# Paged keys and values of a decode step fetched as joined rows of 512 bytes, keys transposed by identity products in column halves, and the prompt outputs' split moved in on-chip memory

## The chip, the cores and the metric

One Trainium2 chip, one of its cores. The metric is the device time of one execution in microseconds. The program uses TensorE (PE, its weight loads PEld), VectorE (DVE), ScalarE (ACT), GpSimd (POOL) and SyncE (SP), which here only issues transfers. SP and POOL each issue transfers to a queue of their own; the core's 16 DMA engines serve both.

## The reference: what is computed

One layer of a hybrid decoder, for a prompt of 512 tokens and for 8 decode batches of 4 new tokens each, all in float32:

```python
hp = pre_mix(xp, ...)            # LN(alpha*x + 0.5*SwiGLU1(x)), 1024 wide, hidden 2816
qa, ka, va, qb, kb, vb, qi, ki, wi = project(hp, w_in[i], ...)
...
o_b = dsa_step(qb, kb, vb, qi, wi, ki, cache_b[i], page_table, bias_b)
xs = post_mix(hs, o_a, o_b, w_out[i], ...)   # w_out, LN, SwiGLU2, LN, gated embedding
```

For the decode tokens, mixer A (12 heads) attends over a cache of 2048 rows per batch (7 blocks of 128 keys are read, `cache_a`), and mixer B (4 query heads, one shared key and value head of 64) attends over those 256 of the past positions that an indexer picks. Mixer B's past is in pages: `cache_b` holds rows of 192 floats, key (64), value (64), indexer key (64), 128 rows to a page, 16 pages to a batch, found by `page_table`. The kernel reads the keys and values of all 128 pages and masks what the indexer left out.

## The kernel before, in words

All five engines run programs written out by hand, synchronised by semaphores; each executes its instructions strictly in the order written. The stages are: the first SwiGLU, the projection (with the indexer's scores), prompt attention (it ends at about 731 us), decode attention (731 to 921 us), `w_out`, the second SwiGLU, the gate. The change lies in decode attention, which has two halves.

**The key half** (731 to 846 us). Mixer A's keys come in 56 blocks `n` of 128 rows by 3072 bytes, 14 for each of four groups `a`. SP issues their loads into a ring of 5 slots (`load_keys`, L489 to L492). After each load from the sixth on it issues one page of mixer B, and two after every fourth, until its 64 pages are out (L518 to L522). POOL issues the 64 pages of odd number one after another (L691 to L692). Both use `load_kv_page` (L375 to L380), which first reads the page's number into a register and then issues one transfer of 64 KB, keys to one half of the tile `kv_b_pages` and values to the other, in runs of 256 bytes. For each block, PE transposes it with six products with the identity (L1998), ACT copies the result to SBUF (L929, L930), and PE takes 12 products with the queries (L1981). PE's loop (L1992 on) transposes block `n` ahead of the scores of block `n - 1`. On DVE the selection of the top 256 runs beside this, cut in pieces with the logits of group `a` after piece `a` (L1432 to L1453):

```python
            for a in range(4):
                if a == 0:
                    list_rounds(0, 16)
                elif a == 1:
                    list_rounds(16, 32)
                    merge_lists()
                    left_per_chunk()
                elif a == 2:
                    mark_rounds(0, 32)
                ...
                dve.wait_ge(S["ka_sc"], 15 * (a + 1))
```

ACT has the softmax exponentials of group `a` in the same loop (`exp_a`, L918, after blocks 18, 32 and 46), so that ACT, and then PE, wait there for DVE's logits.

**The value half** (846 to 917 us). It has 32 steps `v`. Each takes two value blocks of mixer A out of a ring of 7 slots (`values_a`, L2111 on, products on L2124); SP issues a load when two slots are free (L494 to L502). Steps 0 to 15 begin with `transposed_b(v)` (L2005 to L2016): page group `v`, that is page `v` of the 8 batches, is transposed, 4 products of 128x128 with the identity. ACT copies it (`keys_b`, L942), PE takes the scores. Steps 19 to 23 transpose mixer B's probabilities, and steps 24 to 26 are `values_b` (L2085 to L2101): 17 groups of 4 products of 32 output rows, page values against probabilities.

**The prompt's outputs.** Before `w_out` each of the 8 chunks of the prompt's attention output is cast to a rounded part on DVE (`prompt_high`, L1476 to L1479) and the rest is subtracted on POOL (L694 to L699). Both results lie over the pages: the rounded part over the keys (so it waits until all page groups are transposed, `kb_t`), and the last chunk of the rest over a piece of the values (so it waits for `vb_all`, the end of `values_b`). POOL's next work is the first `w_rest` of `w_out` (L557), which waits for ACT's `w_high`; that waits for the last value step (`va_pair`).

Of the kernel before, what the change touches and what calls it, by code (L numbers as in the profile page):

```python
# [22 lines left out]
F32R = mybir.dt.float32r  # L23
# [22 lines left out]
T = SEQ + NDEC  # L46
# [73 lines left out]
def build_program(nc, x_t, p_t, cache_a, cache_b, page_table, ln, kidx_g, kidx_b, w, rel_bias,  # L120
                  rel_rows, consts, onehots, patterns, mask_new, toeplitz, y_t, kv_a_t, a_sample, kv_b_t, ki_b):
    ctx = ExitStack()
    with ctx:
# [4 lines left out]
        def sb(name, shape, dt=F32, at=None):  # L128
# [86 lines left out]
        OT = sb("attn_out_t", [128, KD, T], at=y_at)  # L215
        OH_ = sb("attn_out_high", [128, KD, T], F32R, at=h_at)
        OL_ = sb("attn_out_rest", [128, KD, T], F32R, at=h_at + KD * T * 4)
        SC = sb("idx_scores", [128, CHUNK_COLS + 8], at=e_at)
# [25 lines left out]

        KVP = sb("kv_b_pages", [128, 2, DEC_BATCH * PAGES, HD], at=h_at)
        STA = sb("logits_a", [128, 4, ALL_A], at=h_at + 65536)
# [26 lines left out]
            topk_dec_done kb_t kb_sb kb_sc b_logits b_kept b_max b_exp  # L273
            pt_ps2 pt_a pt_d vb_all ob_sb oa_sb ob_t va_used va_pair ot_done o_tail
            oh_ready o_ready dve_step""".split()
# [99 lines left out]
        def load_kv_page(eng, q):  # L375

            g, b = q // DEC_BATCH, q % DEC_BATCH
            page = eng.value_load(PAGE_IDS[0:1, b * PAGES + g:b * PAGES + g + 1], min_val=0, max_val=cache_b.shape[0] - 1)
            eng.dma_start(KVP[:, :, q, :], cache_b[bass.ds(page, 1), :, 0:2 * HD].rearrange("o p (s n) -> (o p) s n", s=2)  # L379
                          ).then_inc(kv_in[g // 4 + 4 * (q % 2)], 16)  # L380
# [170 lines left out]
        def _(pool):  # L551
# [142 lines left out]
            for c in range(KD):  # L694
                pool.wait_ge(S["oh_ready"], c + 1)
                if c == KD - 1:
                    pool.wait_ge(S["vb_all"], 1)
                nc.gpsimd.tensor_tensor(OL_[:, c, 0:SEQ], OT[:, c, 0:SEQ], OH_[:, c, 0:SEQ].bitcast(F32), ALU.subtract  # L698
                                        ).then_inc(S["o_ready"], 1)  # L699
# [290 lines left out]
        def _(dve):  # L990
# [485 lines left out]
            def prompt_high(c):  # L1476

                dve.wait_ge(S["kb_t"], PAGES)
                v.tensor_copy(OH_[:, c, 0:SEQ], OT[:, c, 0:SEQ]).then_inc(S["oh_ready"], 1)  # L1479

# [100 lines left out]
        def _(pe):  # L1581
# [423 lines left out]
            def transposed_b(g):  # L2005

                if g % 4 == 0:
                    for queue in range(2):
                        pe.wait_ge(kv_in[g // 4 + 4 * queue], 16 * 2 * DEC_BATCH)
                if g >= 2:  # L2010
                    pe.wait_ge(S["kb_sb"], g - 1)
                for p in range(4):
                    last = tr(BANK[2 + g % 2][:, 128 * p:128 * p + 128],
                              KVP[:, 0, DEC_BATCH * g + 2 * p:DEC_BATCH * g + 2 * p + 2, :].rearrange("p b n -> p (b n)"),
                              IDENT)
                last.then_inc(S["kb_t"], 1)  # L2016
# [68 lines left out]
            def values_b(g0, g1):  # L2085
# [5 lines left out]
                for g in range(g0, g1):  # L2091
                    for p in range(4):
                        if g < PAGES:
                            val = KVP[:, 1, DEC_BATCH * g + 2 * p:DEC_BATCH * g + 2 * p + 2, :]
                            probs = PTB[:, g, 32 * p:32 * p + 32]
                        else:
                            val, probs = VBN[:], PTB[0:32, g, 32 * p:32 * p + 32]
                        last = mm(BANK[7][32 * p:32 * p + 32, 0:128], probs, val, start=g == 0, stop=g == PAGES,
                                  skip_group_check=True)
                if g1 == PAGES + 1:  # L2100
                    last.then_inc(S["vb_all"], 1)  # L2101
# [223 lines left out]
```

## Time and profile before

| | |
|---|---|
| time, median of 3 runs | 1476.61 us (1473.54 to 1477.29) |
| the profiled execution's own time | 1477.71 us |
| its span in the trace | 1476.1 us |
| mean granted TensorE clock | 0.972 |
| PE / DVE / ACT / POOL busy | 94% / 38% / 30% / 42% |
| moved by the DMA engines | 269.83 MB, mean 183 GB/s |
| SP's queue / POOL's queue, share of the 16 engines | 51.8% / 2.6% |

PE is busy 94% of the time over the whole program, but the shares are means over stages: in the key half of decode attention PE is busy some three quarters, and other resources decide when the stage ends. The chain of waits over the whole program gives PE 80% and DVE 7%.

### The profile page before, as it was taken

To read this page: it belongs to the slowest core of one execution; us is meant where nothing else is said; L and a number is where in the kernel's file an instruction comes from. 1 tells how busy PE (TensorE), PEld (TensorE's weight loads), DVE (VectorE), ACT (ScalarE), POOL (GpSimd) and SP (SyncE) were. 2 spreads that over 40 slices of the span, in tenths; PEclk is the share of its full clock that TensorE was granted. 3 is DMA by queue.
4 is the path that set the end of the run, shared out by engine and by line. 5 is a ranking of instruction groups with operands and counts; after the bars stand their busy time and mean duration, and the time that the engine had idled before them with its cause. 6 is when DMAs were issued, how large, how long until landed. Compare 5 with 4: busy or idle time off the path is not lost.

```text
span 1476.1 us, 30731 instructions
## 1 busy us (share of the span) xinstructions
PE 1380.6 (94%) x12059; PEld 1272.4 (86%) x12059; DVE 556.1 (38%) x1340; ACT 449.4 (30%) x833; POOL 626.9 (42%) x431
## 2 busy tenths in 40 slices
PE   6999999999989999997876897979999999999988
PEld 6999999999979879965554565969999999999888
DVE  5222222200252346777889524162222222110454
ACT  2122222211252343256643431154222222211441
POOL 6344333455465645221455004534444333544542
PEclk9999999999999999999998998989999999999999
DMA  6299756766355523331299898425565657665221
GB/s 229 79 258 313 271 191 212 252 230 212 117 179 179 150 83 104 133 111 44 61 286 283 247 308 302 143 91 189 172 229 175 220 187 268 218 222 178 72 69 46
DMA packets 95774, 269.83 MB, mean 183 GB/s; under 512 B 36305, under 2 KB 36690, under 8 KB 95160
## 3 DMA queue, kind: packets, MB, share of 16 engines
q1 hardware_dynamic: 89000, 255.34, 51.8%
q0 software_dynamic: 5632, 10.50, 2.6%
q10 hardware_dynamic: 1040, 2.62, 1.2%
q8 instruction: 66, 1.08, 0.3%
q14 instruction: 36, 0.29, 0.1%
HBM read 259.78 MB, written 109.10 MB: 250 GB/s over the span
## 4 chain that ended last, share of the span: by engine, by line
PE 80%; DVE 7%; ACT 4%; POOL 4%; issue 3%; DMA 2%; SPq 1%; ACTq 0%; DVEq 0%; POOLq 0%
PE bank L1588 22%; PE bank L1592 21%; PE bank L1590 21%; POOL w_rest L557 2%; DVE idx_scores L1430 2%; PE bank L2124 2%; PE bank L1941 1%; PE bank L1931 1%; DMA cache_a_ring<-in_cache_a 1%; PE bank L1953 1%; ACT y L785 1%; PE bank L1636 1%; PE bank L1998 1%; DVE idx_scores_left L1376 1%; POOL x_rest L567 1%
## 5 line engine op out<-in xcount | busy, mean ns | idle before, releaser
L557 POOL TENSOR_TENSOR w_rest<-w_raw,w_high 128x1024 fp32r<-128x1024 f32 (+2 forms) x162 | 417.8, 2579 | 593.5 <-ACT w_high L728 592.6
L728 ACT ACTIVATE w_high<-w_raw 128x1024 fp32r<-128x1024 f32 (+2 forms) x162 | 183.5, 1134 | 789.9 <-PE bank L1592 746.5
L1588 PE MATMUL bank<-x_high,w_high 128*128 128x272 f32 x1856 | 388.9, 291 | 15.7 <-POOL x_rest L567 11.6
L1592 PE MATMUL bank<-x_high,w_rest 128*128 128x272 f32 x1856 | 385.4, 289 | 0.0
L1590 PE MATMUL bank<-x_rest,w_high 128*128 128x272 f32 x1856 | 384.1, 289 | 0.0
L1588 PEld LDWEIGHTS bank<-x_high,w_high 128*128 128x128 f32 x1856 | 292.5, 189 | 24.4 <-issue 18.6
L1590 PEld LDWEIGHTS bank<-x_rest,w_high 128*128 128x128 f32 x1856 | 293.0, 189 | 0.0
L1592 PEld LDWEIGHTS bank<-x_high,w_rest 128*128 128x128 f32 x1856 | 291.3, 190 | 0.0
L1032 DVE SCALAR_TENSOR_TENSOR hidden<-silu_gate,bank 128x272 f32<-128x272 f32 x88 | 34.6, 434 | 394.1 <-ACT silu_gate L746 394.1
L1588 PE MATMUL bank<-hidden_high,w_high 128*128 128x272 f32 x616 | 127.8, 289 | 0.0
L1592 PE MATMUL bank<-hidden_high,w_rest 128*128 128x272 f32 x616 | 127.5, 288 | 0.0
L1590 PE MATMUL bank<-hidden_rest,w_high 128*128 128x272 f32 x616 | 127.0, 288 | 0.0
L1588 PEld LDWEIGHTS bank<-hidden_high,w_high 128*128 128x128 f32 x616 | 97.0, 188 | 0.2
L1590 PEld LDWEIGHTS bank<-hidden_rest,w_high 128*128 128x128 f32 x616 | 96.8, 189 | 0.0
L1592 PEld LDWEIGHTS bank<-hidden_high,w_rest 128*128 128x128 f32 x616 | 96.2, 189 | 0.0
L1053 DVE SCALAR_TENSOR_TENSOR y<-y,bank 128x272 f32<-128x272 f32 x42 | 16.5, 434 | 207.6 <-PE bank L1592 179.4
L1998 PE MATMUL bank<-consts_sb,cache_a_ring 128*128 128x128 f32 x336 | 54.4, 304 | 18.5 <-DMA cache_a_ring<-in_cache_a 17.5
L1998 PEld LDWEIGHTS bank<-consts_sb,cache_a_ring 128*128 128x128 f32 x336 | 40.2, 153 | 32.1 <-DMA cache_a_ring<-in_cache_a 24.8
L379 POOL DMA_DIRECT2D kv_b_pages<-in_cache_b x64 | 46.2, 721 | 40.4 <-issue 40.4
L1036 DVE CAST hidden_high<-hidden 128x544 f32 (+1 forms) x44 | 49.1, 1116 | 7.8 <-DVE hidden L1032 3.5
L698 POOL TENSOR_TENSOR attn_out_rest<-attn_out_t,attn_out_high 128x512 fp32r<-128x512 f32 x8 | 10.5, 1329 | 91.8 <-DVE attn_out_high L1479 91.8
L929 ACT ACTIVATE k_a_t<-bank 128x512 f32<-128x512 f32 x56 | 33.4, 597 | 52.7 <-PE bank L1998 52.7
(303 smaller groups left out, 1815.3 us busy)
## 6 DMA issues: line engine op xcount, KB each, us to landing
out_a_sample<-in_cache_a SPq DMA_DIRECT2D x73, 1344.0 KB
w_raw<-in_w_wi SPq DMA_DIRECT2D x88, 512.0 KB, 5.0
cache_a_ring<-in_cache_a SPq DMA_DIRECT2D x112, 384.0 KB, 5.1
w_raw<-in_w_wo SPq DMA_DIRECT2D x32, 704.0 KB, 5.4
w_raw<-in_w_w_in SPq DMA_DIRECT2D x26, 512.0 KB, 3.9
w_raw<-in_w_gate SPq DMA_DIRECT2D x8, 640.0 KB, 3.9
bias_toeplitz<-rev_bias POOLq DMA_DIRECT2D x32, 128.0 KB, 2.7
kv_b_pages<-in_cache_b POOLq DMA_DIRECT2D x64, 64.0 KB, 4.1
```

Source lines behind the costliest of these rows:

```text
L379: eng.dma_start(KVP[:, :, q, :], cache_b[bass.ds(page, 1), :, 0:2 * HD].rearrange("o p (s n) -> (o p) s n", s=2)).then_inc(kv_in[g // 4 + ...
L557: nc.gpsimd.tensor_tensor(WL[:, s, 0:tiles, :], RAW[:, slot, 0:tiles, :], WH[:, s, 0:tiles, :].bitcast(F32), ALU.subtract).then_inc(S["lo_ ...
L728: nc.scalar.activation(WH[:, s, 0:tiles, :], RAW[:, slot, 0:tiles, :], ACT.Copy).then_inc(S["hi_ready"], 1)
L929: nc.scalar.activation(KTA[:, n % 2, 0:512], BANK[b0][:, :], ACT.Copy)
L1032: last = v.scalar_tensor_tensor(half(HF, s, n), half(SG, s, n), 0.5, BANK[4 * s + 2 + n][:, 0:HALF], ALU.mult, ALU.mult)
L1036: v.tensor_copy(HH[:, bass.ds(c, 1), :], HF[:, s:s + 1, :]).then_inc(S["hh_done"], 1)
L1430: own.done(v.match_replace(SC[:], TOP[:, 8 * r:8 * r + 8], SC[:], PASSED))
L1588: mm(banks[n][:, 0:HALF], wh, xh[n], start=start, stop=False)
L1590: mm(banks[n][:, 0:HALF], wh, xl[n], start=False, stop=False)
L1592: last = mm(banks[n][:, 0:HALF], wl, xh[n], start=False, stop=stop)
L1998: last = tr(BANK[2 * (n % 2) + c // 4][:, 128 * (c % 4):128 * (c % 4) + 128], AR[:, n % KEY_RING, 128 * c:128 * c + 128], IDENT)
L2124: last = mm(BANK[a % 2][32 * j:32 * j + 32, 128 * s:128 * s + 128], probs, val, start=k == 0 and i < 4, stop=k == 7, skip_group_check=True)
```

## The change

Each page is now fetched as 128 rows of 512 bytes, key and value together, so the tile has keys and values side by side for every page. A pair of pages' keys is then no longer one block of 128 columns, and the transposition takes each page by itself: 8 products of 64 columns in place of 4 of 128, the two pages of a pair to the lower and the upper 64 rows of the bank. The values of a pair are read as two runs of 64. The parts of the prompt's output lie elsewhere: the rounded part over mixer A's and B's logits (free once they are transposed, `pt_ps2` at 8, at 10 for the last two chunks), the rest over the first 34 pages of the tile (free once `values_b` has done its first six page groups, the new semaphore `vb_part`, on which all 8 chunks wait).

```diff
-        OH_ = sb("attn_out_high", [128, KD, T], F32R, at=h_at)
-        OL_ = sb("attn_out_rest", [128, KD, T], F32R, at=h_at + KD * T * 4)
+        OH_ = sb("attn_out_high", [128, KD, T], F32R, at=h_at + 65536)
+        OL_ = sb("attn_out_rest", [128, KD, T], F32R, at=h_at)
-        KVP = sb("kv_b_pages", [128, 2, DEC_BATCH * PAGES, HD], at=h_at)
+        KVP = sb("kv_b_pages", [128, DEC_BATCH * PAGES, 2 * HD], at=h_at)
-            eng.dma_start(KVP[:, :, q, :], cache_b[bass.ds(page, 1), :, 0:2 * HD].rearrange("o p (s n) -> (o p) s n", s=2)
+            eng.dma_start(KVP[:, q, :], cache_b[bass.ds(page, 1), :, 0:2 * HD].rearrange("o p n -> (o p) n")
                           ).then_inc(kv_in[g // 4 + 4 * (q % 2)], 16)
             for c in range(KD):
                 pool.wait_ge(S["oh_ready"], c + 1)
-                if c == KD - 1:
-                    pool.wait_ge(S["vb_all"], 1)
+                pool.wait_ge(S["vb_part"], 1)
             def prompt_high(c):
-                dve.wait_ge(S["kb_t"], PAGES)
+                dve.wait_ge(S["pt_ps2"], 8 if c < 6 else 10)
                 for p in range(4):
-                    last = tr(BANK[2 + g % 2][:, 128 * p:128 * p + 128],
-                              KVP[:, 0, DEC_BATCH * g + 2 * p:DEC_BATCH * g + 2 * p + 2, :].rearrange("p b n -> p (b n)"),
-                              IDENT)
+                    for e in range(2):
+                        last = mm(BANK[2 + g % 2][64 * e:64 * e + 64, 128 * p:128 * p + 128],
+                                  KVP[:, DEC_BATCH * g + 2 * p + e, 0:HD], IDENT, start=True, stop=True)
-                            val = KVP[:, 1, DEC_BATCH * g + 2 * p:DEC_BATCH * g + 2 * p + 2, :]
+                            val = KVP[:, DEC_BATCH * g + 2 * p:DEC_BATCH * g + 2 * p + 2, HD:2 * HD]
+                if g0 == 0:
+                    last.then_inc(S["vb_part"], 1)
```

How the instructions stand on two engines. First TensorE at the start of the value half (L2082 transposes mixer A's probabilities, L2013 the page keys, L2124 or L2125 takes mixer A's values; the size is that of the output). Before:

```order
L2082 MATMUL bank<-consts_sb,logits_a 32x128
L2013 MATMUL bank<-consts_sb,kv_b_pages 128x128 [waits kv_in4,kv_in0,vnew_in]
L2013 MATMUL bank<-consts_sb,kv_b_pages 128x128 x3
L2124 MATMUL bank<-cache_a_ring,probs_a_t 32x128 [waits ar_in1,ar_in2,pt_d,pt_a]
L2124 MATMUL bank<-cache_a_ring,probs_a_t 32x128 x11
```

With the change:

```order
L2081 MATMUL bank<-consts_sb,logits_a 32x128
L2013 MATMUL bank<-consts_sb,kv_b_pages 64x128 [waits kv_in4,kv_in0,vnew_in]
L2013 MATMUL bank<-consts_sb,kv_b_pages 64x128 x7
L2125 MATMUL bank<-cache_a_ring,probs_a_t 32x128 [waits ar_in1,ar_in2,pt_d,pt_a]
L2125 MATMUL bank<-cache_a_ring,probs_a_t 32x128 x11
```

The place and the waits are the same; 4 products have become 8 of half the rows, in each of 16 steps.

Second, POOL from its last page to the start of `w_out`. Before:

```order
L378 TENSOR_LOAD page_ids
L378 ISA x2
L379 ISA
L379 DMA kv_b_pages<-in_cache_b 128x2x64
L698 TENSOR_TENSOR attn_out_rest<-attn_out_t,attn_out_high 128x512 [waits oh_ready] x7
L698 TENSOR_TENSOR attn_out_rest<-attn_out_t,attn_out_high 128x512 [waits vb_all,oh_ready]
L557 TENSOR_TENSOR w_rest<-w_raw,w_high 128x1024 [waits hi_ready]
```

With the change:

```order
L378 TENSOR_LOAD page_ids
L378 ISA x2
L379 ISA
L379 DMA kv_b_pages<-in_cache_b 128x128
L697 TENSOR_TENSOR attn_out_rest<-attn_out_t,attn_out_high 128x512 [waits vb_part,oh_ready] x8
L557 TENSOR_TENSOR w_rest<-w_raw,w_high 128x1024 [waits hi_ready]
```

The transfer has one run per row in place of two, and the seven subtractions that waited for DVE alone now also wait for the first part of `values_b`.

## Rows read from the trace of the kernel before

**Rows 1.** Chain of waits, 700 to 960 us: start us, us, what.
```profile
745.89 6.77 DMA cache_a_ring<-in_cache_a
...
761.46 0.69 DVE logits_a L1448
...
829.31 0.60 DVE logits_a L1448
```
**Rows 2.** Timeline of DVE, 754 to 765 us: start us, us, instruction [idle before <-releaser].
```profile
756.54 0.71 DVE L1376 MATCH_REPLACE8 idx_scores_left<-topk_lists,idx_scores_left 128x544 f32<-128x544 f32 x1
761.46 0.69 DVE L1448 CUSTOM_DVE_ANT_0 logits_a<-bank,bias_a 128x512 f32<-128x512 f32 x1 [4.21 <-PE bank L1988]
```
**Rows 3.** Timeline of PE, 728 to 762 us: start us, us, instruction [idle before <-releaser].
```profile
740.52 0.87 PE L1998 MATMUL bank<-consts_sb,cache_a_ring 128*128 128x128 f32 x6 [0.95 <-DMA cache_a_ring<-in_cache_a]
...
752.70 1.54 PE L1998 MATMUL bank<-consts_sb,cache_a_ring 128*128 128x128 f32 x6 [2.40 <-DMA cache_a_ring<-in_cache_a]
...
759.63 0.88 PE L1998 MATMUL bank<-consts_sb,cache_a_ring 128*128 128x128 f32 x6
```
**Rows 4.** Timeline of SP's queue, 725 to 850 us.
```profile
736.33 0.70 SPq L492 DMA_DIRECT2D cache_a_ring<-in_cache_a  x1
...
750.52 1.60 SPq L379 DMA_DIRECT2D kv_b_pages<-in_cache_b  x2
752.16 0.58 SPq L492 DMA_DIRECT2D cache_a_ring<-in_cache_a  x1
...
837.95 0.47 SPq L492 DMA_DIRECT2D cache_a_ring<-in_cache_a  x1
```
**Rows 5.** Instructions by tile: durations ns min/median/max, first and last start us.
```profile
L379 POOL DMA_DIRECT2D kv_b_pages<-in_cache_b x64: 720/720/747, 732.9 to 809.6; - x64
L379 SPq DMA_DIRECT2D kv_b_pages<-in_cache_b x64: 377/378/848, 734.7 to 839.2; - x64
...
L355 SPq DMA_DIRECT2D idx_pages_ring<-in_cache_b x64: 337/338/672, 444.7 to 581.6; - x64
...
L355 POOL DMA_DIRECT2D idx_pages_ring<-in_cache_b x64: 534/537/700, 463.9 to 590.4; - x64
```
**Rows 6.** Stretches: PE, PEld, DVE, ACT, POOL busy, PEclk, DMA share, GB/s.
```profile
735.00:740.00 5.00, 4.57 (x66) 3.21 (x58) 4.76 (x11) 3.41 (x8) 2.89 (x4) 1.00 0.75 216
...
745.00:750.00 5.00, 3.66 (x51) 2.62 (x51) 4.79 (x10) 1.98 (x5) 3.29 (x5) 1.00 1.05 284
750.00:755.00 5.00, 2.60 (x26) 1.74 (x20) 4.76 (x12) 1.36 (x4) 2.18 (x3) 0.71 0.95 293
...
885.00:890.00 5.00, 4.41 (x72) 3.09 (x75) 2.61 (x9) 1.16 (x2) 0.00 (x0) 1.00 0.99 348
```
**Rows 7.** Timeline of ACT, 801 to 833 us.
```profile
830.73 1.07 ACT L920 ACTIVATE logits_a<-logits_a,small 128x928 f32<-128x928 f32 x1 [4.70 <-DVE small L1452]
```
**Rows 8.** Timeline, 725 to 760 us: half-array and full-array products in prompt attention.
```profile
727.31 0.66 PE L1953 MATMUL bank<-probs_t,kv_b_tok 128*64 128x128 f32 x8
...
727.90 1.09 PE L1941 MATMUL bank<-consts_sb,logits 128*128 128x128 f32 x8
```
**Rows 9.** Timeline of PE, 846 to 884 us.
```profile
849.42 0.66 PE L2013 MATMUL bank<-consts_sb,kv_b_pages 128*128 128x128 f32 x4
```
**Rows 10.** Timeline of all engines, 884 to 924 us.
```profile
898.92 5.46 POOL L698 TENSOR_TENSOR attn_out_rest<-attn_out_t,attn_out_high 128x512 fp32r<-128x512 f32 x4 [2.92 <-DVE attn_out_high L1479]
...
911.42 1.26 POOL L698 TENSOR_TENSOR attn_out_rest<-attn_out_t,attn_out_high 128x512 fp32r<-128x512 f32 x1 [0.36 <-DVE attn_out_high L1479]
...
917.73 2.34 POOL L557 TENSOR_TENSOR w_rest<-w_raw,w_high 128x1024 fp32r<-128x1024 f32 x1 [5.05 <-ACT w_high L728]
```
**Rows 11.** Instructions by tile: mixer B's values.
```profile
L2098 PE MATMUL bank<-kv_b_pages,probs_b_t x128: 272/273/273, 899.4 to 905.4; 128*32 128x128 f32 x128
```
**Rows 12.** Landing of the keys' and values' loads.
```profile
DMA to landing us min/median/max: 3.2/5.1/6.9
```
**Rows 13.** Timeline of PE, 884 to 924 us: the end of the value half.
```profile
913.59 1.51 PE L2124 MATMUL bank<-cache_a_ring,probs_a_t 128*32 128x128 f32 x24 [2.81 <-DMA cache_a_ring<-in_cache_a]
```

More of the change, by code:

```diff
@@ L273, in build_program @@
             topk_dec_done kb_t kb_sb kb_sc b_logits b_kept b_max b_exp
-            pt_ps2 pt_a pt_d vb_all ob_sb oa_sb ob_t va_used va_pair ot_done o_tail
+            pt_ps2 pt_a pt_d vb_part vb_all ob_sb oa_sb ob_t va_used va_pair ot_done o_tail
             oh_ready o_ready dve_step""".split()
```

## The prediction

> **What bounds the kernel now.** The page sends one to decode attention, since the change touches nothing else; I read the chain of waits there first. It runs through one landing of mixer A's keys, then through DVE's top-256 selection from 761 to 829 us, broken only by the logits of each group [rows 1]. So three places could matter: the key loads up to 761 us, DVE's own chain after them, and the tail of the value half.
>
> The first place has the only slack I can find for this change. DVE ends its first 16 list rounds at 756.54 + 0.71 = 757.25 us and then stands idle 4.21 us for the scores of group 0 [rows 2]. PE is late with them because it waits for keys: block 6 starts 0.95 us late, block 11 has waited 2.40 us [rows 3]. After that gap PE's blocks 11 to 13 run at the lower clock level (1.2 GHz for part of the time; the granted clock of 750 to 755 us is 0.71 [rows 6], and six transposes take 1.54 us in place of 0.88 [rows 3]). Two things hold the keys back. SP's queue has a pace of its own: keys 6 and 14 are issued at 736.33 and 752.16 us, 1.98 us a block, since most of a page's issue is the read of its number (two pages take 1.60 us) [rows 4]. And the DMA engines are full: share 0.75 at 735 us, 1.05 at 745 us, for 284 GB/s, while the value half, which moves only long rows, gets 348 GB/s at share 0.99 [rows 6]. Pages in runs of 256 bytes are the difference in the mix.
>
> **The change part by part.**
>
> *Runs of 512 bytes.* Half the descriptors. On POOL a page costs 720 ns with 256 runs and 537 ns with 128 [rows 5]; on SP 378 and 338 ns [rows 5]. SP issues 12 pages ahead of key 14, so this key is issued 12 x 0.04 = 0.5 us sooner, at 751.7 us. Landing: key 6, issued while the engines were at 0.75, was used 740.52 - 736.33 = 4.2 us later [rows 3, 4]; the median of all ring loads is 5.1 us, the fastest 3.2 us [rows 12]. From PE's start on block 14 to DVE's logits it takes 761.46 - 759.63 = 1.83 us at the full clock [rows 2, 3], because block 13's scores come after block 14's transposes. So DVE would start at 751.7 + landing + 1.83:
> - landing 3.2 us: 756.7 us, before DVE asks. All 4.2 us go.
> - landing 4.2 us: 757.7 us, gain 3.7 us.
> - landing 5.1 us: 758.6 us, gain 2.8 us.
> - nothing lands sooner and the low clock stays: only the 0.5 us of issue.
>
> I take between the two middle rows, 4.6 us and a gain of 3.3 us: the mix becomes cheaper, so I expect the queue to stay nearer to its state of 735 us, and the gap of 2.40 us, with the low clock behind it, to shrink. Bounds: 0.5 and 4.2 us.
>
> The Trainium skill, DMA: Bandwidth & Descriptors, Specifications, puts the least transfer at line rate at 512 bytes and says that below it the engine does a read-modify-write. By it the whole penalty of the pages goes and the 4.2 us are taken; no row shows a run of 512 bytes, and the pair of shares above only agrees in direction.
>
> *Faster issue on POOL.* It gives 64 x 0.183 = 11.7 us back to an engine that waits for nobody there. But its pages press on the engines sooner: one each 0.96 us in place of 1.14 us, so 26 in place of 22 over the 25 us to 757 us. Four pages are 262 KB, at 284 GB/s 0.9 us of engine time taken from the keys. I count it inside the landing times above, and keep 0.9 us as the bound of a loss.
>
> *What is late next.* A shift of DVE at 757 us carries on only if nobody else is late. From 761 to 829 us DVE itself is the chain, without a gap [rows 1], and ACT waits for it 4.70 us before the exponentials of group 2 at 830.73 us [rows 7], with PE behind ACT. SP ends its last key at 837.95 us [rows 4]; it saves 64 x 0.04 = 2.6 us on its pages, and what it waited for PE after 801 us shrinks with DVE's shift, so it keeps step with 3.3 us. The half-clock restart of PE after 831 us stays, as the stall that causes it stays. The value half then starts 3.3 us sooner, with the same loads and the same work.
>
> *Transposes in halves.* 16 groups, 4 full-array products replaced by 8 half-array ones, at the same place. Four full ones are busy 0.66 us [rows 9], eight in alternating halves 0.66 us, eight full ones 1.09 us [rows 8]: two halves together cost one full product, (1.09 - 0.66) / 4 = 0.11 us. Cost 0, within 16 x 0.05 = 0.8 us either way. If the halves did not overlap, each group would cost 4 x 0.11 = 0.43 us more, 6.9 us in all, on PE, which is the bound of that stretch.
>
> The Trainium skill speaks against this edit. TensorEngine Tiling (Array Packing), Gotcha 2, says that tiling by columns excludes fast weight load and, for fp32, the transpose mode, and TensorE: Matmul & The Clock Gate, Terms, calls that mode four times faster for fp32. By that rule the eight would be four times dearer than the four. In the rows just named the trace does not agree: full transposes and half-array products move the same columns in the same time.
>
> *Page values as two runs of 64.* Another layout of the moving operand, at 128 products that take 6.0 us in all [rows 11]. No row shows such an operand; if it halved their rate it would cost up to 6 us in steps 24 to 26, beside a tail in which PE waits for landings anyway (2.81 us in one place [rows 13]). I take 0, bounds 0 to 3.
>
> *The split of the prompt outputs.* DVE's casts: at their place in DVE's program the eighth transposition group of mixer A has been taken already, the new wait costs nothing. POOL's eight subtractions now start at `vb_part`, about 901 us, the end of the first part of `values_b`. Before, four took 5.46 us from 898.92 us, and the last ended at 912.68 us [rows 10]. Now six in a row take 6 x 1.37 = 8.2 us, to 909.2 us, and the seventh and eighth wait for DVE as before, until 912.7 us. Behind them is the first `w_rest`, which starts at 917.73 us after 5.05 us of idling [rows 10]. Cost 0 with 5 us in hand; DVE's casts at 899 us lose their neighbour on POOL, which nobody waits for.
>
> *Sum.* 1477.7 - 3.3 = 1474.4 us against the profiled execution's own time. That lies 1.1 us over the median of the three runs, so against the median it is 1473.3; I say 1473.5 us. What a measurement of this kernel can tell from no change is 0.3%, 4.4 us.
>
> **The rivals.**
> 1. *More than DVE's wait comes back.* With the wait gone (4.2 us), the halves a little faster (0.8 us) and PE never late in the key half, one stretch of low clock less might show at its end: at the lower level six transposes cost 0.66 us more (1.54 for 0.88 [rows 3]) and the scores of a block some 0.4 us by the same ratio, so two blocks 2 us. Gain 7 us, 1469.5 us. For it: each of the key waits stems from full engines. Against: DVE's chain caps what the key half can give at 4.2 us, and a PE that is early stalls longer, so its clock falls all the same.
> 2. *SP's pace is the whole matter.* Landings are 4 to 5 us whatever the engines' load, or POOL's sooner pages take what the longer runs give (0.9 us), or the engines take two keys' worth of 256 bytes as fast as one of 512, so that the edit does not do what it says. Then 0.5 us of gain less 0.9 us of loss: 1476 to 1477 us. For it: 1.98 us a block is SP's pace. Against: the gap of 2.40 us is no matter of pace, since key 11 was issued in time.
> 3. *The halves do not overlap, slower.* Place: L2013, PE's bound stretch from 847 to 883 us. Price: 6.9 us if the products queue, 16 x 0.7 = 11 us if their weight loads show too. The tail is full of transfers, so nothing of it is taken back there. With the gain of the key half taken off, 1480 to 1485 us. It decides slower from 8 us of price on, or with no gain in the key half from 4.4 us. For it: the weight of each half changes with every product, and the values' strided operand adds to it. Against: prompt attention has the same pattern at the same size [rows 8].
>
> **How the numbers follow.** The forecast (gain 1.5 to 4.8 us) has 0.55, rival 1 0.24, rival 2 0.13, rival 3 0.08. The predicted time is the forecast's. The range is 1470.5 to 1477.5 us: the lower end takes in the full 4.2 and the 0.8 us (1471.6) and the near part of rival 1, the upper end rival 2 with its 0.9 us of loss; rival 3 and the far part of rival 1 are left out. Faster by over 0.3%: rival 1 and the forecast's edge, 0.27. Within 0.3%: the rest of the forecast and rival 2, 0.65. Slower: 0.08.
>
> **What would show it.** POOL's page issue at about 540 ns and SP's at 340 ns; DVE's wait before the logits of group 0 down from 4.21 to about 1 us; the gap before block 11 below 1 us, with the granted clock of 750 to 760 us near 1; the value half starting about 3 us sooner; L2013 eight products in 0.6 to 0.7 us. The prediction is wrong if the wait of group 0 stays above 3 us, if the groups of L2013 last 1 us or more, if ACT's wait before 830 us vanishes (then SP or PE has become the bound), or if POOL's last subtraction ends after the first `w_high`.

## The result and the profile after

The change runs in 1481.26 us, the median of 8 runs (1478.29 to 1483.89), against 1475.63 us (1472.56 to 1477.29) for the kernel before in 8 runs on the same chip. The ratio is 1.0039, with a 95% interval of 1.0023 to 1.0054, so the change is **slower**, by 5.6 us between the medians. The predicted 1473.5 us had the wrong sign, and the range (to 1477.5 us) missed. The profiled execution took 1482.50 us, its span is 1480.8 us, the mean granted clock 0.971.

I cut decode attention at three points of PE's timeline in each trace: the first transposition of mixer A's keys, the first transposition of its probabilities (the end of the key half), and the first product of `w_out`. Before they stand at 731.62, 846.25 and 921.08 us, after at 732.47, 844.31 and 924.65 us. The key half went from 114.63 to 111.84 us, the value half from 74.83 to 80.34 us. So the loss lies in the value half. The 2.8 us of the key half look like the gain that was predicted, but kernels with the same key half differ by as much from one execution to the next (the table further down), so this pair of traces alone doesn't show it.

PE's timeline after, at the start of the value half (start us, us, instruction):

```profile
845.33 1.09 PE L2013 MATMUL bank<-consts_sb,kv_b_pages 128*64 128x128 f32 x16
...
847.49 1.09 PE L2013 MATMUL bank<-consts_sb,kv_b_pages 128*64 128x128 f32 x16
848.51 0.86 PE L2125 MATMUL bank<-cache_a_ring,probs_a_t 128*32 128x128 f32 x24
```

The number behind the x, the count of rows, is what I had not reckoned with. A page group has 8 products in the program and 16 rows in the trace, and it takes 848.51 - 847.49 = 1.02 us. The group of before, 4 products in 4 rows, takes 850.01 - 849.42 = 0.59 us to the next start; that is the row of [rows 9] and the one behind it:

```profile
850.01 0.86 PE L2124 MATMUL bank<-cache_a_ring,probs_a_t 128*32 128x128 f32 x24
```

The views of the instructions by tile (durations in ns, minimum, median and maximum, then the first and the last start) say it for all 16 groups. First before, then after:

```profile
L2013 PE MATMUL bank<-consts_sb,kv_b_pages x64: 272/273/330, 847.2 to 882.5; 128*128 128x128 f32 x64
```

```profile
L2013 PE MATMUL bank<-consts_sb,kv_b_pages x256: 272/273/323, 845.3 to 887.4; 128*64 128x128 f32 x128
...
L2097 PE MATMUL bank<-kv_b_pages,probs_b_t x128: 272/273/273, 906.0 to 912.3; 128*32 128x128 f32 x128
L379 POOL DMA_DIRECT2D kv_b_pages<-in_cache_b x64: 544/547/568, 733.7 to 808.2; - x64
L379 SPq DMA_DIRECT2D kv_b_pages<-in_cache_b x64: 336/338/947, 735.5 to 837.5; - x64
```

64 products left 64 rows, 128 products left 256. The stretch from the first to the last group grew from 35.3 to 42.1 us, by 6.8 us or 0.43 us a group. The 128 value products with their strided operand have the same 273 ns. The page issues fell from 720 and 378 ns [rows 5] to 547 and 338 ns, as forecast from the index pages' rows.

POOL's timeline, before and after, shows what the shorter issue is worth (each row with the idle time before it):

```profile
738.97 0.72 POOL L379 DMA_DIRECT2D kv_b_pages<-in_cache_b  x1 [0.45 <-issue]
740.12 0.72 POOL L379 DMA_DIRECT2D kv_b_pages<-in_cache_b  x1 [0.42 <-issue]
```

```profile
738.64 0.55 POOL L379 DMA_DIRECT2D kv_b_pages<-in_cache_b  x1 [0.60 <-issue]
739.79 0.55 POOL L379 DMA_DIRECT2D kv_b_pages<-in_cache_b  x1 [0.61 <-issue]
```

One page each 1.15 us in both at this place: what the issue gives, the gap ahead of it takes. Over all 64 pages the mean is 1.22 us before and 1.18 us after (first to last start 76.7 and 74.5 us). The wait of DVE for the scores of group 0, 4.21 us before [rows 2], is 2.27 us after:

```profile
760.37 0.69 DVE L1447 CUSTOM_DVE_ANT_0 logits_a<-bank,bias_a 128x512 f32<-128x512 f32 x1 [2.27 <-PE bank L1987]
```

By stretches, the granted clock (the first number after the last bracket, 0.81 and 0.85), the busy share of the DMA engines and their GB/s:

```profile
750.00:755.00 5.00, 3.12 (x34) 2.07 (x32) 4.76 (x11) 1.61 (x4) 2.51 (x5) 0.81 0.98 311
755.00:760.00 5.00, 5.00 (x81) 3.82 (x78) 3.00 (x6) 2.42 (x7) 2.42 (x5) 0.85 0.96 311
```

Two signs that the prediction had named did not come: this clock was to be near 1, and the wait ahead of key block 11 below 1 us, where it was 1.88 us (2.40 us before):

```profile
752.86 1.36 PE L1997 MATMUL bank<-consts_sb,cache_a_ring 128*128 128x128 f32 x6 [1.88 <-DMA cache_a_ring<-in_cache_a]
```

At the other end, POOL's subtractions came later than before and still had room:

```profile
907.68 7.43 POOL L697 TENSOR_TENSOR attn_out_rest<-attn_out_t,attn_out_high 128x512 fp32r<-128x512 f32 x6 [98.89 <-PE bank L2097]
...
917.20 1.26 POOL L697 TENSOR_TENSOR attn_out_rest<-attn_out_t,attn_out_high 128x512 fp32r<-128x512 f32 x1 [0.36 <-DVE attn_out_high L1478]
921.30 2.34 POOL L557 TENSOR_TENSOR w_rest<-w_raw,w_high 128x1024 fp32r<-128x1024 f32 x1 [2.84 <-ACT w_high L727]
```

The first `w_rest` still waits for ACT's `w_high`, 2.84 us, not for POOL's own work.

### The profile page after: what moved, and what is told of

Read it like the earlier page. It is cut to its first block, busy times and chain, and to the rows that moved or that the text cites. A ratio compares the mean times of both kernels' runs of the same rounds, so it can differ in the third digit from the quotient of the medians.

```text
span 1480.8 us, 31122 instructions
## 1 busy us (share of the span) xinstructions
PE 1389.1 (94%) x12251; PEld 1283.3 (87%) x12251; DVE 553.5 (37%) x1340; ACT 449.7 (30%) x833; POOL 615.9 (42%) x431
## 4 chain that ended last, share of the span: by engine, by line
PE 81%; DVE 8%; POOL 4%; ACT 3%; issue 2%; DMA 2%; SPq 0%; ACTq 0%; DVEq 0%; POOLq 0%
PE bank L1587 22%; PE bank L1591 21%; PE bank L1589 21%; POOL w_rest L557 2%; DVE idx_scores L1429 2%; PE bank L2125 2%; DMA cache_a_ring<-in_cache_a 1%; PE bank L1940 1%; PE bank L1635 1%; PE bank L2013 1%; PE bank L1952 1%; PE bank L1930 1%; PE bank L1636 1%; PE bank L1637 1%; PE bank L1997 1%
## 5 line engine op out<-in xcount | busy, mean ns | idle before, releaser
L379 POOL DMA_DIRECT2D kv_b_pages<-in_cache_b x64 | 35.0, 547 | 49.1 <-issue 49.1
```

The lines of the kernel that those rows point to most:

```text
L379: eng.dma_start(KVP[:, q, :], cache_b[bass.ds(page, 1), :, 0:2 * HD].rearrange("o p n -> (o p) n")).then_inc(kv_in[g // 4 + 4 * (q % 2)], 16)
```

## The experiments

Times are medians; each ratio is against runs of the kernel before on the same chip, with its 95% interval. A gain or a loss in us is worked out from the ratio, unless two medians are named; with few runs the two can differ.

**The three parts, each alone.** These four ran together, beside 29 runs of the kernel before at 1475.32 us.

`e1_halves_alone`: the kernel before with its transpositions in halves, from the old layout.

```diff
-                    last = tr(BANK[2 + g % 2][:, 128 * p:128 * p + 128],
-                              KVP[:, 0, DEC_BATCH * g + 2 * p:DEC_BATCH * g + 2 * p + 2, :].rearrange("p b n -> p (b n)"),
-                              IDENT)
+                    for e in range(2):
+                        last = mm(BANK[2 + g % 2][64 * e:64 * e + 64, 128 * p:128 * p + 128],
+                                  KVP[:, 0, DEC_BATCH * g + 2 * p + e, :], IDENT, start=True, stop=True)
```

> The kernel before, with its own page layout and 256-byte runs; only the 64 full transposes become 128 products of 64 columns with the identity. Theory A (a plain float32 product runs as two passes and a transpose as one, so a group costs 1.02 us for 0.59 us; 16 x 0.43 = 6.9 us on TensorE, of which the value half takes back some 1.4 us): slower by 5.5 to 6.9 us, DVE's wait for group 0 still 4.2 us, L2013 with 256 rows. Rival B (the products are hidden, the loss comes from the moved outputs or the strided values): within 1.5 us of before.

Measured: 1484.51 us (6 runs), 1.0049 [1.0031, 1.0067], 7.2 us slower with an interval of 4.6 to 9.9 us; the medians lie 9.2 us apart. The trace has 256 rows for the 128 products, from 845.7 to 887.8 us, 42.1 us as in the change. The whole loss is this one edit. DVE's wait for group 0 was 3.73 us here.

`e2_rows_alone`: the change, with four full-array transposes of a whole page's row of key and value in place of the halves. It leaves out the keys of the odd pages and keeps the strided values and the moved outputs.

```diff
-                    for e in range(2):
-                        last = mm(BANK[2 + g % 2][64 * e:64 * e + 64, 128 * p:128 * p + 128],
-                                  KVP[:, DEC_BATCH * g + 2 * p + e, 0:HD], IDENT, start=True, stop=True)
+                    last = tr(BANK[2 + g % 2][:, 128 * p:128 * p + 128],
+                              KVP[:, DEC_BATCH * g + 2 * p, :], IDENT)
```

> The changed kernel, but with 4 full transposes to a group again, each of the 128 neighbouring columns of the even page (its keys and its values); the odd pages' keys are left out, so the time and not the output is that of joined rows with the old cost on TensorE. Theory A: faster than before by 2 to 3.5 us, the value half from the transposes of mixer A's probabilities to w_out as long as before (74.8 us). Rival B: as slow as the change, or no gain over before.

Measured: 1474.12 us, 0.9988 [0.9977, 0.9999], 1.8 us faster. Instructions by tile:

```profile
L2012 PE MATMUL bank<-consts_sb,kv_b_pages x64: 272/273/330, 844.5 to 879.9; 128*128 128x128 f32 x64
```

The stretch is 35.4 us again. So the fetch in rows of 512 bytes, with the two other parts beside it, is a gain of about half the size I had put on it. The interval runs from 0.1 to 3.4 us: the sign is just clear of noise, the size is not well known.

`e3_moved_alone`: the kernel before with only the prompt outputs moved and their waits changed.

```diff
-        OH_ = sb("attn_out_high", [128, KD, T], F32R, at=h_at)
-        OL_ = sb("attn_out_rest", [128, KD, T], F32R, at=h_at + KD * T * 4)
+        OH_ = sb("attn_out_high", [128, KD, T], F32R, at=h_at + 65536)
+        OL_ = sb("attn_out_rest", [128, KD, T], F32R, at=h_at)
...
-                if c == KD - 1:
-                    pool.wait_ge(S["vb_all"], 1)
+                pool.wait_ge(S["vb_part"], 1)
...
-                dve.wait_ge(S["kb_t"], PAGES)
+                dve.wait_ge(S["pt_ps2"], 8 if c < 6 else 10)
```

> The kernel before with only the prompt outputs' split moved and its waits changed as in the change. Theory A: within 0.5 us of before, POOL's last subtraction 3 us or more ahead of the first w_rest. Rival B: slower by 1 to 2 us, after decode attention (the two traces differ by 1.1 us there) or at its end.

Measured: 1475.71 us, 0.9998 [0.9986, 1.0011]: nothing, within 2 us. Its trace holds a second finding. Its key half is the code of the kernel before, and yet DVE's wait for group 0 is not 4.21 us:

```profile
759.64 0.69 DVE L1447 CUSTOM_DVE_ANT_0 logits_a<-bank,bias_a 128x512 f32<-128x512 f32 x1 [0.89 <-PE bank L1987]
```

The stretch ahead of it, with the granted clock at 1.00 where [rows 6] has 0.71:

```profile
750.00:755.00 5.00, 3.05 (x40) 2.17 (x39) 4.76 (x12) 1.74 (x4) 2.30 (x4) 1.00 0.98 310
```

So a part of the 4.21 us on which the forecast rested belongs to that execution, not to the kernel. Why one execution has the dip and another not stays open; PE had waited 2.40 us for block 11 ahead of it in one, 1.82 us in the other.

`e4_pool_pages_later`: the kernel before, POOL's pages held back until the scores of group 0 are taken.

```diff
             pool.wait_ge(S["o_sb"], 8)
+            pool.wait_ge(S["ka_sc"], 15)
             for q in range(1, DEC_BATCH * PAGES, 2):
```

> The kernel before; POOL waits for the scores of group 0 before its first page, so that its 64 pages leave the engines free from 733 to 760 us. Theory C (full DMA engines hold the first keys): landings of keys 6 to 14 near 4 us, DVE's wait of 4.2 us down to 1 us or less, 3 to 4 us faster. Rival D (SP's own pace of 1.98 us a block holds them): DVE's wait stays above 3 us and the time is the same; TensorE then waits before key blocks as often as before.

Measured: 1475.13 us, 0.9999 [0.9986, 1.0011]. With no page of POOL's on the engines until then, DVE still waited 0.70 us, much as in `e3_moved_alone` with all of them. The wait fell, as the one theory had it, and the time stayed, as its rival had it, so shortening this wait by itself is not enough. A gain of under 2 us can't be told from none here, and the pages held back press on the engines later.

**What a half costs.** The next three ran together, beside 28 runs of the kernel before at 1475.75 us.

`e7_transposes_twice`: the kernel before, each full-array transpose done twice.

```diff
-                    last = tr(BANK[2 + g % 2][:, 128 * p:128 * p + 128],
+                    for _ in range(2):
+                        last = tr(BANK[2 + g % 2][:, 128 * p:128 * p + 128],
```

> The kernel before with each of the 64 full transposes done twice, 8 to a group, and nothing else. Theory A (TensorE's time here goes by passes: one for a full transpose, two for a plain product, two halves at once): a group takes 1.02 us, as with the 8 half products (16 rows in the trace), and the time is that of halves alone, 5 to 8 us slower. Rival (half products cost more than their passes, by weight loads or tiling): at most 3 us slower, groups under 0.9 us.

Measured: 1481.21 us, 1.0040 [1.0025, 1.0055], 5.9 us slower. PE's timeline:

```profile
852.63 1.09 PE L2014 MATMUL bank<-consts_sb,kv_b_pages 128*128 128x128 f32 x8
853.66 0.86 PE L2125 MATMUL bank<-cache_a_ring,probs_a_t 128*32 128x128 f32 x24
```

Eight transposes leave 8 rows and take 1.03 us, to the start of the next row: a transpose is one row each, and doubling them costs what the halves cost.

`e8_even_halves_only`: the change without the products of the odd pages.

```diff
-                    for e in range(2):
+                    for e in range(1):
```

> The changed kernel with only the even page's product of each pair, 4 plain half products to a group; the odd pages' keys are left out. Theory A (the two halves of a pair run at once, each product is two passes): a group still takes 1.0 us and the time is that of the changed kernel. Rival G (the halves do not overlap, a product costs one pass of 0.11 us more than nothing, and eight of them 1.02 us): a group takes 0.6 us and the time falls by 5 to 7 us to the level of before.

Measured: 1480.83 us, 1.0036 [1.0023, 1.0050], 5.3 us slower, as slow as the change with half its products. PE's timeline:

```profile
853.02 1.09 PE L2013 MATMUL bank<-consts_sb,kv_b_pages 128*64 128x128 f32 x8
854.04 0.86 PE L2125 MATMUL bank<-cache_a_ring,probs_a_t 128*32 128x128 f32 x24
```

Four half-array products leave 8 rows and take 1.02 us; the change's eight leave 16 rows and take 1.02 us too. So two halves side by side do overlap fully. What doubles is something else: each plain product, the identity ones among them, stands as two rows and takes the time of two. I call such a row a pass, and the time of one pass in a full pipeline a slot, (1.03 - 0.59) / 4 = 0.11 us by `e7_transposes_twice`. Four plain products of two passes cost what eight transposes of one do.

Is that the price of a plain product or of one half of the array? No run puts a plain product on the full array in place of a transpose, but the kernel before has one. `bias_b` in the value half takes a single plain product of all 128 rows against 512 columns (L2028), and it too leaves two rows:

```profile
850.80 1.12 PE L2028 MATMUL bank<-onehots_b,rel_b 128*128 128x512 f32 x2
851.86 0.42 PE L2048 MATMUL bank<-k_b_t,q_b_blocks 128*32 128x128 f32 x8
```

It takes 1.06 us to the next start, about as long as eight transposes of 128 columns. So the two rows, and their time, come without halves too.

`e5_fewer_sp_pages`: the kernel before with 32 pages on SP, from block 15 on, and 96 on POOL (the counts of the semaphores, changed to match, are left out here).

```diff
-                while page_at < min(64, (5 * (n - 4) + 3) // 4):
-                    load_kv_page(sp, 2 * page_at)
+                while n >= 15 and page_at < min(32, (4 * (n - 14) + 4) // 5):
+                    load_kv_page(sp, 4 * page_at)
...
-            for q in range(1, DEC_BATCH * PAGES, 2):
-                load_kv_page(pool, q)
+            for q in range(DEC_BATCH * PAGES):
+                if q % 4:
+                    load_kv_page(pool, q)
```

> The kernel before (256-byte runs, full transposes), but SP issues only 32 pages, from key block 15 on, and POOL 96 from 733 us on. Theory E (SP's queue, with its page issues of 1.2 us, paces the keys and ends them late: last page at 839.2 us before, 836.1 us in the run with joined rows alone, which was 1.8 us faster): DVE's wait for group 0 at 0, SP's last key issue several us before 838 us, value loads starting sooner against the first value step; 2 to 4 us faster. Rival F (in the key half DVE's own chain is all that counts, and its wait varies with TensorE's clock from one execution to the next, 0.9 to 4.2 us in the traces of kernels that are the same there): within 1.5 us of before.

Measured: 1474.30 us, 0.9989 [0.9979, 1.0000]: 1.6 us of gain, between 0 and 3.1 us. DVE's wait for group 0 was gone altogether, and ACT's timeline shows where it went, first before, then here:

```profile
802.43 1.07 ACT L920 ACTIVATE logits_a<-logits_a,small 128x928 f32<-128x928 f32 x1 [6.89 <-DVE small L1452]
```

```profile
799.38 1.07 ACT L921 ACTIVATE logits_a<-logits_a,small 128x928 f32<-128x928 f32 x1 [15.61 <-DVE small L1453]
...
827.68 1.07 ACT L921 ACTIVATE logits_a<-logits_a,small 128x928 f32<-128x928 f32 x1 [5.63 <-DVE small L1453]
```

Keys that come earlier only make ACT, and PE behind it, wait longer for DVE's logits: 15.61 us in place of 6.89 us ahead of the exponentials of group 1. That stop takes back what quicker keys give.

**Taking the cap away.** The last four ran together, beside 29 runs of the kernel before at 1476.31 us. In each, ACT does the exponentials of group 1 after key block 44 instead of 32 and those of group 2 in the value half.

```diff
-                if n >= 18 and (n - 18) % 14 == 0:
-                    exp_a((n - 18) // 14)
+                if n in (18, 44):
+                    exp_a((n - 18) // 26)
...
-                if v == 2:
-                    exp_a(3)
+                if v in (1, 2):
+                    exp_a(v + 1)
```

`e9_exps_later`: this edit in the kernel before.

> The kernel before with two of ACT's exponentials moved: that of group 1 from key block 32 to 44, that of group 2 from block 46 to the second value step. TensorE then no longer stands behind ACT and DVE at blocks 35 and 49. Theory H (in the key half DVE's selection is the bound through these two waits, so quicker pages can give little): the key half (first transpose to the first transpose of mixer A's probabilities, 111 to 115 us so far) falls by 3 to 5 us, now paced by SP and the engines, and the whole by 3 to 5 us. Rival: the value half's loads take it back (they share the engines with SP's last pages): under 1.5 us.

Measured: 1475.94 us, 1.0001 [0.9987, 1.0014]: nothing, where 3 to 5 us were expected.

`e10_exps_later_fewer_sp_pages`: this edit and that of `e5_fewer_sp_pages`.

> The exponentials moved as in the run before this one, and pages as in the run with 32 of them on SP and 96 on POOL. Theory H: with DVE's waits and SP's pace both gone the engines bound the key half (30.4 MB at some 300 GB/s, 101 us): key half 101 to 106 us, 6 to 10 us faster than before. Rival: no more than the exponentials alone give.

Measured: 1462.51 us (6 runs), 0.9904 [0.9883, 0.9925], 14 us faster than the kernel before and the best of all kernels here. That is more than the 6 to 10 us expected: the expectation had the DMA engines stop the key half at some 300 GB/s, and from 735 to 800 us they moved 326 GB/s. The idle time of PE and PEld that ended with a landing of mixer A's ring (us, times), in `e9_exps_later`, then in `e10_exps_later_fewer_sp_pages`:

```profile
  DMA cache_a_ring<-in_cache_a: 70.6, 82
```

```profile
  DMA cache_a_ring<-in_cache_a: 29.8, 59
```

The kernel before has 46.9 us in 51 waits there. With the exponentials out of the way but 64 pages on SP, PE waits for keys instead, since SP's issue of keys and pages has its own pace; the chain of waits of `e9_exps_later` from 725 to 930 us runs through it (shares by line; on SP's queue L492 issues keys, L378 and L379 read a page's number and issue the page):

```profile
by line: DMA cache_a_ring<-in_cache_a 14.3%; SPq L379 10.3%; PE bank L2124 9.8%; SPq L378 9.7%; SPq L492 8.5%; issue 7.8%; PE bank L1998 5.3%; PE bank L2013 4.3%; DMA w_raw<-in_w_w_out 3.4%; PE bank L1981 2.5%; PE bank L1588 2.4%; PE bank L
```

Its key half took 113.03 us. With both edits it took 827.70 - 732.75 = 94.95 us, and PE then met the third bound, DVE's selection:

```profile
827.70 1.97 PE L2083 MATMUL bank<-consts_sb,logits_a 128*128 128x128 f32 x8 [6.54 <-DVE small L1453]
829.46 1.06 PE L2014 MATMUL bank<-consts_sb,kv_b_pages 128*128 128x128 f32 x4
```

The value half, 78.76 us, is 3.9 us longer than before; it starts at the lower clock (1.06 us for four transposes). Two bounds held the key half side by side, so that lifting either one showed almost nothing and lifting both showed 14 us.

`e11_change_exps_later`: the edit in the change.

> The changed kernel with the exponentials moved. Theory A and H: its loss on TensorE (16 x 0.43 us) stays, its gain in the key half grows, since now transfers and SP pace that half: 2 to 4 us slower than the kernel before with the exponentials moved, against 5.8 us without.

Measured: 1477.55 us, 1.0009 [0.9994, 1.0025]. That is 1.6 us over the median of `e9_exps_later`, somewhat less than the 2 to 4 us expected.

`e12_rows_alone_exps_later`: the edit in `e2_rows_alone`.

> Joined rows of 512 bytes alone (full transposes, the odd pages' keys left out) with the exponentials moved. Theory H: 3 to 5 us faster than the kernel before with the exponentials moved, more than the 1.8 us that the rows gave where DVE capped the key half. Rival: again 2 us or less, since SP's pace and not the engines holds the keys.

Measured: 1472.16 us, 0.9973 [0.9962, 0.9984]. Two differences are read from these. The last two kernels differ by the halves alone: 1477.55 - 1472.16 = 5.4 us, the price of the halves once more. And `e12_rows_alone_exps_later` against `e9_exps_later` is the rows alone with ACT's stop out of the way: 3.8 us between the medians in place of 1.8 us. By the intervals of the two ratios the 3.8 us hold to some 2.6 us either way, so it is not shown that the rows are worth more there. The traces agree in direction, with key halves of 109.16 us (`e12_rows_alone_exps_later`) and 107.69 us (`e11_change_exps_later`) against 113.03 us. A kernel with the two edits of `e10_exps_later_fewer_sp_pages` and rows of 512 bytes was not tried.

## Why the prediction was wrong

The parts add up within their intervals. The halves gave +7.2 us and all the rest, `e2_rows_alone` with the moved outputs in it, -1.8 us; that makes 5.4 us, and 5.6 us were measured. (Between medians it is 9.2 - 1.2 = 8.0 us, with only six runs behind the 9.2.) By the traces (milestones as above, us; the stretch is from the first to the last page transposition; the last columns are the GB/s and the busy share of the DMA engines from 735 to 800 us, and their quotient):

| kernel | key half | value half | stretch | GB/s | share | GB/s by share |
|---|---|---|---|---|---|---|
| before | 114.63 | 74.83 | 35.3 | 283 | 0.95 | 298 |
| the change | 111.84 | 80.34 | 42.1 | 285 | 0.91 | 313 |
| `e1_halves_alone` | 113.33 | 84.04 | 42.1 | 277 | 0.93 | 298 |
| `e2_rows_alone` | 110.62 | 72.42 | 35.4 | 292 | 0.93 | 314 |
| `e3_moved_alone` | 111.11 | 75.78 | 36.1 | 278 | 0.94 | 296 |
| `e7_transposes_twice` | 111.93 | 81.48 | 41.6 | 280 | 0.94 | 298 |
| `e8_even_halves_only` | 110.50 | 83.66 | 41.9 | 283 | 0.90 | 314 |

The stretch tells the two groups apart without exception: 35 to 36 us with 64 transposes, 42 us with the halves or twice the transposes. The key and the value half themselves scatter by some microseconds, each being one execution, with dips of the clock at other places.

**Transposes in halves: the step that failed.** I wrote that "eight in alternating halves" take 0.66 us, from [rows 8], and that "two halves together cost one full product", so cost 0 within 0.8 us. The row of L1953 says x8, and I took it for 8 products. The code of prompt attention has two products for each key block up to the diagonal, so 2, 4, 6 or 8 in a step. The last four steps, in the trace before:

```profile
724.38 0.44 PE L1953 MATMUL bank<-probs_t,kv_b_tok 128*64 128x128 f32 x4
...
727.31 0.66 PE L1953 MATMUL bank<-probs_t,kv_b_tok 128*64 128x128 f32 x8
...
728.92 1.90 PE L1953 MATMUL bank<-probs_t,kv_b_tok 128*64 128x128 f32 x28
```

Two products leave 4 rows, four leave 8, six and eight together 28. So the x8 are the four products of a step with two blocks: 8 passes, overlapped two by two, in 0.66 us. Over the whole of prompt attention L1953 has 160 products and 320 rows, L1941 160 transposes and 160 rows. The row was evidence for the price, read as evidence against it. The same slip stands in the words on the kernel before: a key block has 6 products with the queries (L1981), not 12; 12 is the number of their rows. Read rightly, eight halves are 16 passes, 8 slots, and L1941's x8, 1.09 us in the same [rows 8], gives their time to the hundredth. The check I skipped was to count the instructions of that step in the program against the rows of the trace; [rows 9] with x4 for 4 transposes would have set the other side.

The Trainium skill had it right here, and I set it aside: TensorEngine Tiling (Array Packing), Gotcha 2, excludes the transpose mode for fp32 under tiling by columns. The traces agree in so far as the halves stood as two rows each where the transposes stood as one; whether a transpose could be kept in a half of the array no run tried. The factor of four that the Trainium skill, TensorE: Matmul & The Clock Gate, Terms, gives for that mode is not what they show: the passes doubled, and a group went from 0.59 to 1.02 us.

**Rival 3** had the place (L2013, PE's bound stretch), the price (6.9 us against 0.43 x 16 = 6.9 us) and the time (1480 to 1485 us), but not the mechanism: it said that the halves do not overlap, and `e8_even_halves_only` shows that they do. That its price fitted is no merit, since a doubling of passes and a loss of overlap give the same number; only leaving out half of the products tells them apart. It had a chance of 0.08 because of the misread row. Its "nothing of it is taken back" in the tail was nearly right: from the last page transposition to `w_out` the change has 924.65 - 887.4 = 37.3 us against 921.08 - 882.5 = 38.6 us, so 1.3 us came back.

**Runs of 512 bytes: the right sign, too large.** The forecast was 3.3 us; the run gave 1.8 us. It was worked out against a wait of 4.21 us in one execution. In the table's four traces with the old fetch the waits are 4.21, 3.73, 1.98 and 0.89 us, mean 2.7 us; in the three with the new fetch 2.27, 1.25 and 0.96 us, mean 1.5 us. The key halves of the same traces have means of 112.75 and 110.99 us, 1.8 us apart. With such a scatter, from a single execution each, these means go the same way as `e2_rows_alone` and prove nothing by themselves.

The reason behind the step is borne out in direction, its size is not. The last column of the table parts the two fetches: scaled to a busy share of 1, the engines moved 296 to 298 GB/s with runs of 256 bytes and 313 to 314 GB/s with runs of 512, 5% more (`e9_exps_later` has 299, `e11_change_exps_later` and `e12_rows_alone_exps_later` 314 and 318). These kernels issue the same loads in the same order up to 800 us. Where the order differs the quotient does too, 293 in `e4_pool_pages_later` and 318 in `e5_fewer_sp_pages`, so it is a comparison and no price. And the landings of the ring's loads, on which the sum was built, do not part them: their medians are 5.1, 4.6, 5.0 and 4.5 us with the old fetch (the rows of the table in order) and 4.7, 4.8 and 4.5 us with the new. The forecast had taken 4.6 us as what the longer runs bring, against 5.1 us, and the old fetch has it too. The Trainium skill's rule of 512 bytes (DMA: Bandwidth & Descriptors, Specifications) gave 4.2 us here, and no run shows so much: 1.8 us, and 3.8 us with ACT's stop moved.

**Faster issue on POOL: wrong reason, no harm to the sum.** "One each 0.96 us in place of 1.14 us" did not come: 1.15 us in both, 1.22 and 1.18 us over all pages. So there was next to no earlier pressure on the engines, and `e4_pool_pages_later` shows no effect of it on the time.

**What is late next** held: ACT still waited before its exponentials of group 2. That it was 4.70 us as in [rows 7], to the hundredth, is chance: the other traces of the table have 3.44 to 5.40 us. `e5_fewer_sp_pages` turned this wait into the larger finding.

**Page values as two runs of 64** cost nothing that shows, as taken: 273 ns each, and 6.3 us from the first to the last against 6.0 us [rows 11]. **The split of the prompt outputs** cost nothing within 2 us (`e3_moved_alone`). POOL's last subtraction ended at 918.5 us, not at 912.7 us, since `values_b` itself came later; of the 5.05 us in hand [rows 10] 2.84 us were left.

## What to carry to other kernels

Before a group of rows in a trace is taken as a price for so many products, count the products in the program: a float32 product may stand there as two rows, a float32 transpose as one, and an operation that looks alike in shape costs twice as much. A wait in one trace is a sample; look at the same wait in a second execution before you count on it as a gain. And where two bounds lie close together, test them in pairs: here each alone gave 0 to 1.6 us and both 14 us.

## What the runs showed of the hardware

- A plain float32 product against 128 columns stands as two rows of 273 ns each (a slot of about 0.11 us in a full pipeline) and takes the time of two float32 transposes, which stand as one row each: 64 transposes left 64 rows, 128 transposes 128, 64 plain half products 128, 128 plain half products 256. A plain product on the full array against 512 columns left two rows too, in 1.06 us.
- Products on the two column halves of the array, issued in turn, overlap fully: 8 in 1.02 us, and 4 of one half alone also in 1.02 us.
- Halving the runs of a page's transfer shortened POOL's issue from 720 to 547 ns and left its period at 1.15 us where it was read (1.22 and 1.18 us over all pages).
- Scaled to the same busy share, the DMA engines moved 313 to 314 GB/s with page runs of 512 bytes and 296 to 298 GB/s with 256, in the same mix with rows of 3072 bytes and the same order of loads.
- The same code at the same place saw a granted clock of 1.00 in one execution and 0.71 in another, and a wait of 0.89 or 4.21 us behind it. The two do not always go together: `e7_transposes_twice` had 1.00 and 1.98 us, and `e8_even_halves_only`, with the new fetch, 0.70 and 0.96 us.
